# Three transformer layers on one core: spreads issued in mid-tile, small steps regrouped, and the first two out projections in rounds over pairs of inputs

## The reference, cut to what matters

```python
memn = rms_norm(mem, mem_norm_w)
for layer in range(2):
    u = rms_norm(x, attn_norm_w[layer]) @ w_in[layer]            # 1024 -> 2560
    if layer == 0:   # chunked retention, 6 heads, group norm, silu gate
        o_main = silu(g) * rms_norm(retention(q, k, v), ret_gn_w)
    else:            # differential attention: two softmax maps a head
        q, k = rms_norm(q, ...), rms_norm(k, ...)
        o = softmax(q0 k0) - lam * softmax(q1 k1), times v
        o_main = rms_norm(o, diff_subln_w) * (1 - lambda_init)
    o_mem = memory_attention(rms_norm(qc), rms_norm(mk), mv)     # mk, mv from memn @ w_mem_kv
    x = x + concat(o_main, o_mem) @ w_out[layer]                 # 1024 -> 1024
    h = rms_norm(x, ffn_norm_w[layer]) @ w_gate_up[layer]        # 1024 -> 2 * 2816
    x = x + (silu(h[:2816]) * h[2816:]) @ w_down[layer]
# layer 2: Mamba-2 scan (16 heads, 4-tap convolution) beside forgetting attention (16 heads)
proj = rms_norm(x, norm_mix_w) @ w_in_2                          # 1024 -> 5664
x = x + concat(ssd_mixer(...), fox_mixer(...)) @ w_out_2         # 2048 -> 1024
x = x + (silu(gate) * val) @ w_down_2   # gate, val = conv3(rms_norm(x) @ w_up_2)
```

## Time and profile before

| | before |
|---|---|
| median of three runs | 1100.18 us (1098.59 to 1103.19) |
| the profiled execution's own time | 1097.26 us |
| its span in the profile | 1095.5 us |
| PE busy | 1052.4 us, 96% |
| DVE busy | 760.9 us, 69% |
| ACT busy | 586.6 us, 54% |
| POOL busy | 178.8 us, 16% |
| mean granted clock of TensorE | 0.995 of full |
| read from HBM | 172.39 MB |

### The profile page before, as it was taken

One profiled execution on the slowest core, in us unless ns is written; L12 is line 12 of the kernel. 1 busy time (PEld: TensorE's weight loads), 2 busy tenths in 40 slices (PEclk: granted clock), 3 DMA queues, 4 the chain that ended last, 5 costly groups with the idle time before them and its releaser, 6 DMA issues.

```text
span 1095.5 us, 23936 instructions
## 1 busy us (share of the span) xinstructions
PE 1052.4 (96%) x8666; PEld 1013.2 (92%) x8666; DVE 760.9 (69%) x1323; ACT 586.6 (54%) x1047; POOL 178.8 (16%) x186
## 2 busy tenths in 40 slices
PE   5999999999999998999999999989899999999998
PEld 5989999999999877899999999988788999999998
DVE  6876686666555887866666459857877679988843
ACT  6654564444544645654445446655555566666532
POOL 4100121111110000411111110000212023444300
PEclk9999999999999999999999999999999999999999
DMA  7533455555565321555555654433232455555563
GB/s 279 179 134 106 144 175 185 180 180 179 178 194 165 124 88 53 189 178 186 184 180 176 194 184 141 172 115 136 78 116 71 133 196 179 175 188 176 167 208 103
DMA packets 51480, 174.45 MB, mean 159 GB/s; under 512 B 5840, under 2 KB 7120, under 8 KB 51280
## 3 DMA queue, kind: packets, MB, share of 16 engines
q1 hardware_dynamic: 51408, 173.46, 47.5%
HBM read 172.39 MB, written 1.05 MB: 158 GB/s over the span
## 4 chain that ended last, share of the span: by engine, by line
PE 80%; DVE 14%; ACT 3%; issue 2%; POOL 1%; DMA 1%; SPq 0%; DVEq 0%; POOLq 0%; ACTq 0%
PE bank L678 23%; PE bank L679 23%; PE bank L680 23%; DVE ring_lo L1447 4%; DVE xw_lo L1453 1%; ACT tmp L1212 1%; PE bank L663 1%; PE bank L665 1%; PE bank L664 1%; PE bank L788 1%; ACT tmp L1269 1%; PE bank L879 1%; PE bank L977 1%; DVE root_parts L1651 1%; PE bank L899 1%
## 5 line engine op out<-in xcount | busy, mean ns | idle before, releaser
L678 PE MATMUL bank<-xw_hi,ring_hi 128*128 128x256 f32 x1576 | 452.0, 287 | 2.6 <-ACT lam L1347 1.1
L679 PE MATMUL bank<-xw_lo,ring_hi 128*128 128x256 f32 x1576 | 446.0, 283 | 0.0
L680 PE MATMUL bank<-xw_hi,ring_lo 128*128 128x256 f32 x1576 | 445.8, 283 | 0.0
L1447 DVE TENSOR_TENSOR ring_lo<-ring_raw,ring_hi 128x1024 fp32r<-128x1024 f32 (+2 forms) x338 | 402.3, 1194 | 57.9 <-ACT ring_hi L1031 52.2
L1031 ACT ACTIVATE ring_hi<-ring_raw 128x1024 fp32r<-128x1024 f32 (+2 forms) x338 | 341.2, 1012 | 90.5 <-PE bank L680 84.5
L678 PEld LDWEIGHTS bank<-xw_hi,ring_hi 128*128 128x128 f32 x1576 | 302.3, 192 | 8.3 <-issue 3.7
L679 PEld LDWEIGHTS bank<-xw_lo,ring_hi 128*128 128x128 f32 x1576 | 302.4, 192 | 0.2
L680 PEld LDWEIGHTS bank<-xw_hi,ring_lo 128*128 128x128 f32 x1576 | 302.3, 192 | 0.0
L678 PE MATMUL bank<-act_hi,ring_hi 128*128 128x256 f32 x736 | 211.6, 288 | 11.0 <-DVE ring_lo L1853 7.5
L679 PE MATMUL bank<-act_lo,ring_hi 128*128 128x256 f32 x736 | 209.3, 284 | 0.0
L680 PE MATMUL bank<-act_hi,ring_lo 128*128 128x256 f32 x736 | 209.2, 284 | 0.0
(11 more groups left out here) (193 smaller groups left out, 1180.6 us busy)
## 6 DMA issues: line engine op xcount, KB each, us to landing
ring_raw<-w_up SPq DMA_DIRECT2D x132, 512.0 KB, 3.2
ring_raw<-w_in SPq DMA_DIRECT2D x85, 512.0 KB, 3.2
ring_raw<-w_down SPq DMA_DIRECT2D x48, 512.0 KB, 3.5
ring_raw<-w_down SPq DMA_DIRECT2D x24, 384.0 KB, 3.8
ring_raw<-w_ob SPq DMA_DIRECT2D x10, 512.0 KB, 3.8
ring_raw<-w_oa SPq DMA_DIRECT2D x16, 256.0 KB, 2.6
ring_raw<-w_oa SPq DMA_DIRECT2D x8, 512.0 KB, 3.6
ring_raw<-w_kv SPq DMA_DIRECT2D x7, 512.0 KB, 6.9
```

What stands on the lines that cost most here:

```text
L678: mm(bank[b][:, 0:T], w_hi, tile(hi, t), start=kk == 0, stop=False)
L679: mm(bank[b][:, 0:T], w_hi, tile(lo, t), start=False, stop=False)
L680: last = mm(bank[b][:, 0:T], w_lo, tile(hi, t), start=False, stop=end)
L1447: V.tensor_tensor(ring_lo[:, a:b], ring_raw[:, a:b], ring_hi[:, a:b].bitcast(f32), SUB).then_inc(lo_done, 1)
```

## The change

Seven things are changed.

1. In layers 0 and 1 the phases oa and ob become one phase oc of eight rounds (`project_rounds`). Round (pair, half) multiplies one pair of inputs into four outputs; the order is (0,0), (1,0), (0,1), (1,1), (2,0), (2,1), (3,0), (3,1), with the pairs (6,7), (0,1), (2,3), (4,5). All eight sums lie two to a bank in banks 0 to 3, and x gets them in four additions of 512 columns in rounds 6 and 7.
2. In layer 1 most spreads, in layer 2 all spreads and `ssd_out`, are issued in the middle of the next tile (`amid`). Spreads of layer 1 named `spread_soon` stay where they were. In DVE's EARLY list of those layers `ssd_skip` and `norm_out` come last.
3. `ssd_out` reads one of four buffers (`ssd_w`), so ACT may be two pairs ahead.
4. At the start ACT splits kv tile 1 before the first square; POOL adds six squares, PE itself sums the last two, after kv tile 2; kv weights are split one tile further ahead, and three tiles of x are split before the kv loop.
5. Plan: gate_silu and gated of layer 0 one slot earlier, the last norm of layer 1 one slot earlier, its last mixes at slot 25.
6. Lambda's sums and exponential move to slot 1 of layer 0.
7. `small_r` holds its 256 columns in doubled order (512 columns, in `act_hi`), so that the broadcasts of the scan and of the forgetting attention take one matmul of 384 columns and not two of 256 and 128.

```diff
-          ("in0", 20, [8], 20), ("oa0", 8, [6], 8), ("ob0", 2, [8], 2), ("up0", 44, [8], 4), ...
-          ("in1", 20, [8], 20), ("oa1", 8, [4], 8), ("ob1", 4, [8], 4), ("up1", 44, [8], 4), ...
+          ("in0", 20, [8], 20), ("oc0", 8, [8], 8), ("up0", 44, [8], 4), ...
+          ("in1", 20, [8], 20), ("oc1", 8, [8], 8), ("up1", 44, [8], 4), ...
+ROUNDS = [(0, 0), (1, 0), (0, 1), (1, 1), (2, 0), (2, 1), (3, 0), (3, 1)]
...
-        plan[layer][slot + 2].insert(0, ("spread", tile))
+        plan[layer][slot + 2].insert(0, ("spread_soon" if soon or slot >= 20 and layer == 1 else "spread", tile))
...
-    norm(1, 23, 10 + 64, True)
+    norm(1, 22, 10 + 64, True)
...
         def ssd_w(h):
-            return tmp[:, 1920 + (h % 2) * 384:2304 + (h % 2) * 384]
+            room, a = (tmp, 1920) if h % 4 < 2 else (con, CCOL["dist"])
+            return room[:, a + (h % 2) * 384:a + 384 + (h % 2) * 384]
...
+        X_SPLITS = {1: (3,), 2: (4, 5), 3: (6,), 4: (7,)}
+        X_SQUARES = {1: (0, 1), 2: (2, 3), 3: (4, 5), 4: (6, 7)}
...
+            def project_rounds(layer, then, halfway):
+                ph = PH[f"oc{layer}"]
+                for c, (pair, half) in enumerate(ROUNDS):
+                    slot, g = ph.tile(0, c)
+                    pe.wait_ge(lo_done, g + 1)
+                    ...
+                    for j in range(4):
+                        if j == 2:
+                            halfway(c)
+                        m = 4 * half + j
+                        b = m // 2
+                        ...
+                        o = bank[b][:, (m % 2) * T:(m % 2) * T + T]
+                        for k in range(2):
+                            t = ph.inputs[2 * pair + k]
+                            if m == 0:
+                                pe.wait_ge(mix_lo, number["mix", (layer, t)] + 1)
+                            ...
+                        if pair == 3 and j == 1:
+                            last.then_inc(ob_done, 1)
+                    last.then_inc(tile_done, 1)
+                    then(c)
...
+                if q == 0:
+                    mm(bank[7][:, 0:T], cmat("ones1024"), sqsum, start=True, stop=False)
+                    pe.wait_ge(sq_done, KT)
+                    for r in (KT - 2, KT - 1):
+                        last = mm(bank[7][:, 0:T], cmat("ones1024"), two(sq, r % 2), start=False, stop=r == KT - 1)
...
-                    if c == (1 if name == "kv" else 0) and q is not None:
+                    if c == (2 if name == "kv" else 0) and q is not None:
                         mean_square(q)
...
-                    for it, a, width in blocks_:
-                        mm(bank[2 + n][:, a:a + width], pick, small_r[:, 0:width], start=it == 0, stop=False)
+                    mm(bank[2 + n][:, 0:T + P], pick, small_r[:, 0:T + P], start=True, stop=False)
...
+            HALFWAY = ((), ("spread",), ("spread", "ssd_out"))
...
-                if layer == 1:
-                    pe.wait_ge(lam_in, 1)
-                    mm(bank[5][:, 0:2], ...).then_inc(lam_ps, 1)
-                    pe.wait_ge(lam_e, 1)
...
             for g in range(1, AHEAD):
                 split_hi(PH["kv"], 0, g - AHEAD)
-                for m in range(3 * g - 1, 3 * g + 2):
+                for m in range(4 * g - 4, 4 * g):
                     stream_square(0, m, u)
+                    for k in {5: (0, 1), 6: (2,)}.get(m, ()):
+                        act.wait_ge(x_loaded, 16)
+                        stream_hi(1, k, x)
...
+            def rounds_into_stream(layer, q, early, middle, late):
+                ph = PH[f"oc{layer}"]
+                for c in range(ph.n):
+                    early(ph, 0, c)
+                    if c >= 6:
+                        for p in (2 * c - 12, 2 * c - 11):
+                            ...
+                            V.tensor_tensor(two_out, two_out, bank[p][:, :], ADD).then_inc(out_ready, 1)
+                            if p:
+                                stream_lo(q, 2 * p - 2, x)
+                                stream_lo(q, 2 * p - 1, x)
+                    ...
+                    split_lo(ph, 0, c)
+                    late(ph, 0, c)
```

229 lines of the change are left out of this document (153 added, 76 removed), and 4 rows, old and new, of the table PHASES.

## The result

| | before | changed |
|---|---|---|
| median of five runs each, us | 1100.18 (1098.43 to 1103.19) | 1088.51 (1086.83 to 1090.04) |
| ratio | | 0.9891, 95% interval 0.9868 to 0.9913 |
| profiled execution, us | 1097.26, span 1095.5 | 1086.83, span 1085.0 |
| PE busy, us | 1052.4 | 1050.0 |
| PE idle, us | 43.1 | 35.0 |

The change is faster by 11.7 us in the medians (10.5 in the profiles). I had predicted 1077 us, a gain of 21.6, with a range that ended at 1088. The direction was right, and about half of the gain is missing.

A forecast was written before the change was run, and what follows sets the result against it. PE was taken to bound the kernel, busy 1052.4 of 1095.5 us. Gains of 1.5 + 3.8 + 1.1 + 5.2 + 2.3 + 6.5 + 1.2 = 21.6 us took the profiled 1097.26 to 1075.7; median predicted 1077, range 1070 to 1088.

The forecast's parts named there:

- The start, 1.5: Kv phase: without PE's wait for POOL's sums, kv tile 3 starts at 21.0, not 22.5; gain 1.5 us, bounds 0 and 2.7.
- Out projection of layer 0, 3.8: Start of layer 0's out projection: a 2.08 us wait for split inputs and a 1.7 us clock loss go; gain 3.8 us.
- Up0 stays as it is: Start of layer 0's up projection: unchanged within 0.7 us either way, wide additions saving DVE a little, later order costing a little.
- Lambda, 1.1: Start of layer 1: PE's wait for lambda goes as its work moves to layer 0; gain 1.1 us, lower bound 0.
- Layer 1, 5.2: Layer 1: spreads 3.4, softmax 1.4, clock 0.9, mixes 0.5, less about 1.0 at up1; net gain 5.2 us, bounds 1.5 and 9.5.
- The clock, 3.5 in three terms: Half-speed stretches in layers 0, 1 and 2: gains of 1.7, 0.9 and 0.9 us from less slow clock, 3.5 in all.
- the clock stays: Rival: all three half-speed stretches return, 3.5 us less gain, 1080.5 us; chance 0.10.
- Layer 2, 10.0: Layer 2: 2.3 us from the long `ssd_out` wait and clock, 6.5 from other `ssd_out` and spread waits, 1.2 from broadcasts.
- Broadcasts, 1.2: Layer 2's broadcasts: merging the attention's matmuls saves 0.15 us for each of eight head pairs, 1.2 us; bounds 0 and 1.5.
- Slower by the half tile as DVE's wait: Rival: 23 deferred steps in layers 1 and 2 each give PE its bank up to 1.44 us later; worst 1123 us; chance 0.05.
- DVE takes over: Rival: in layers 1 and 2 waits return behind DVE's one queue, 7.0 us less gain, 1084 us; chance 0.18.
- Rounds still wait for mixes: Rival: layer 1's rounds wait for late mixes, each wait bringing a clock stretch, 6.4 us less gain, 1083 us; chance 0.07.

The follow-up runs named there:

- u_kv: m_all4 with the start as before (splits and squares of x beside the first four kv tiles, POOL summing all eight squares); 1077.01 us.
- c_lo: Changed kernel with DVE's low half of the weight tile in round 6 computed ahead of that round's two additions, layers 0 and 1; 1085.26 us.
- f_half1: Changed kernel with layer 1's spread matmuls back at the end of their tile; 1091.63 us.
- a_bank: Changed kernel with the out projection rounds' four PSUM banks taken in order 1, 0, 2, 3, in both layers; 1087.57 us.
- b_mix: Changed kernel with layer 1's mixes of head pair 2, 3 put ahead of the last RMS norm's root in slot 23; 1086.33 us.
- d_all: Changed kernel with the edits of a_bank, b_mix and c_lo together; 1079.71 us.
- o_fill: Changed kernel with 18 unused matmuls filling PE's waits in the first tile of up0 and of up1; 1086.68 us.
- t_bcast: m_all4 with layer 2's broadcasts, for decays and attention, in two matmuls each again; 1075.45 us.
- s_ssdend: k_nosort with layer 2's `ssd_out` back at the tile's end, its spreads still in mid-tile; 1096.75 us.
- k_nosort: Changed kernel with DVE's early steps of layer 2 in the plan's order, `norm_out` no longer sorted to the end; 1083.92 us.
- m_all4: Changed kernel with all four repairs: the edits of a_bank, b_mix, c_lo and k_nosort; 1074.24 us.
- j_norounds_bank: Changed kernel with both out projections by output as before, first output in the bank the last input tile has not used; 1086.91 us.
- g_half2: Changed kernel with layer 2's spreads and `ssd_out` back at the end of their tile; 1099.29 us.
- h_kv: Changed kernel with the start as before (splits and squares of x beside the first four kv tiles, POOL summing all eight squares); 1091.66 us.

## Why the prediction was wrong

By the two marks and the spans, in us of the profiled executions (with the repairs the marks stand at 340.40 and 650.10, the span is 1072.6):

| | forecast | changed | with the four repairs |
|---|---|---|---|
| start and layer 0, lambda among it | 6.4 | 2.9 | 5.4 |
| layer 1 | 5.2 | -1.5 | 4.4 |
| layer 2 | 10.0 | 9.1 | 13.1 |
| sum | 21.6 | 10.5 | 22.9 |
| of it clock | 3.5 | 0 | 5.1 |

The time fell the way that was forecast, but by 11.7 us and not 21.6, and landed just above the range. Two things failed: the terms of layer 1 and of the start of up0, which left out what stands ahead in the other engines' queues, and the clock's 3.5 us, of which none came. With the four repairs the waits give 17.8 us without the clock, against 18.1 forecast, so the places for the gain were there.

- **The start, 1.5.** By the first spread 0.8 (48.47 to 47.69). Mis-sized, inside its bounds. Kv tile 3 began at 21.31, near the 21.0 of the sum; what I had not seen is a wait of 0.57 for a low part at 36.97 that before did not have. On medians the new start is worth 2.8 to 3.2, since the wait that it removes can bring stretches of slow clock; in the one run of u_kv with a granted clock of 1.00 it is 0.7.
- **Out projection of layer 0, 3.8.** Oc0 began without the wait and without the stretch, as said. What failed is "Up0 stays as it is": from its first matmul to the mean it took 6.8 us (140.19 to 146.97) against 4.5. The order of DVE's queue in round 6, which I had put at "within 0.7 either way", cost more than half of the term, and a stretch came there. c_lo shows it: start and layer 0 are 2.3 us shorter with the order changed, 1.7 of it that stretch.
- **Lambda, 1.1.** Right: the row is gone.
- **Layer 1, 5.2, the step that failed.** It lost 1.5. The softmax's wait went to 0.3, better than the 1.0 of the sum. Its spreads were worth 1.5 and not 3.4, by f_half1 without the clock; the median's 3.1 is near by luck. The half tile of cover took the spreads' waits away, but one of them, 1.83, came back as the norm's 1.90. Three more things were wrong. I had not looked at which bank round 0 begins in (2.3 us). I let the mixes wait 0.5 and they waited 2.0: not POOL's 3.41 us was at fault but the norm ahead of the mixes in ACT's queue, put there by the slot that the change moved the norm to. And up1's first tile took 7.0 us (456.99 to 463.99), not 4.5. These last three are shown by a_bank, b_mix and c_lo together, d_all: layer 1 falls from 315.7 to 309.7 us.
- **The clock, 3.5 in three terms.** Three stretches went and three came. The rival "the clock stays" had this right with its 3.5 us. The Trainium skill ("TensorE: Matmul & The Clock Gate", HAM oscillation) describes an array that falls back in the waits between groups of matmuls. Every stretch here did follow waits, and in o_fill none came where they were filled; the stretches at 411 and 424 show that a wait alone does not tell whether one comes.
- **Layer 2, 10.0.** 9.1 by the marks, and near by luck: two errors cancel. On the medians the mid-tile steps are worth 14.0 and not the 8.8 that I gave them, but 5.0 of it is clock; the rest, 9.1, is near the 7.9 of the sum (1.4 + 6.5). The sort of DVE's list, which I had not priced at all, cost 4.0 by the marks (4.6 on the medians). My sum of separate waits, 2.3 for `ssd_out` and 6.5 for the rest, is not how they divide: spreads alone bring nothing that is clear of noise.
- **Broadcasts, 1.2.** Right as a sum, by t_bcast; by the rows 0.10 a pair and not 0.15. By the Trainium skill's issue gap alone it would have been 0.1 ("TensorE: Matmul & The Clock Gate", Back-to-back issue gap), and the same section says that this formula under-counts for matmuls of few columns, since it leaves out the loading of the weights; the measured 1.2 decides for the rows.
- **Rivals.** "Slower by the half tile as DVE's wait" did not come. "DVE takes over" is seen as a mechanism in s_ssdend, in the norm's 1.90 us of layer 1 and in the norms' waits behind the sorted list, but the last comes by the order of its queue and not by DVE being full: k_nosort and m_all4 have the same work on DVE and no such wait in layer 2. "Rounds still wait for mixes" had the right place in layer 1, with 2.0 us and a stretch. "The clock stays" was right about the clock, and its 1080.5 wrong since it kept the other terms.
- **What was to show it.** PE busy fell by 2.4, within 5; the idle time is 35 and not 25; the spreads' rows are under 2.5 and `ssd_out` under 2. Kv tile 3 began without the wait of about 1 that I had named.

What stays open: why the same wait has a stretch at half speed in one run and none in another, what `ssd_out` in mid-tile brings without the spreads, and whether rounds or the old order are better in layer 1 once both have the right bank.

## What to carry to other kernels

When work is regrouped on the engine that sets the time, write down for each boundary what the other engines have in their queues just before the first thing that it needs: the bank it starts in, the norm ahead of its mixes, the weight split between its sums. The four losses that were repaired here were each one thing in the wrong place, a bank or an order in a queue; none was missing throughput. Waits on one queue move: here moving one of two steps that depend on the same engine brought nothing clear of noise, since the other's waits grew by about as much, and moving both brought 9.1 us, 14.0 with the clock. And compare variants by the marks of the part that was edited, beside the granted clock: medians that differ by one or two stretches can point the wrong way, as in j_norounds_bank.

## What the runs showed of the hardware

- A stretch at half speed was 3.4 us long or twice that, and took 1.7 or 3.4 us from PE. The profiles of the change and its eighteen variants have between none (m_all4) and seven (g_half2, h_kv) of them, a long one counted twice, behind single waits of 1.06 to 3.32 us or rows of short ones, the least of them 0.36 and three of 0.26 (u_kv at 456 us; m_all4 has the same row and no stretch).
- A stretch that took 1.7 us from PE cost the kernel nothing where a wait for DVE stood behind it (t_bcast, 408 to 412 us). An edit in one layer moved stretches in another: k_nosort, whose layers 0 and 1 are those of the changed kernel, has twice the stretch at 145 to 151 us. With up to 1.7 us per stretch, the medians of neighbouring variants tell less than the marks in their traces. The five runs of m_all4 agreed within 0.5 us, at granted clocks of 1.00 and 0.998.
- DVE's low part of a weight tile (128x1024) took 1.77 us at 139.41 and 1.23 us at 133.18; in the first case POOL was adding squares (138.40 to 141.75). In c_lo it moved to a time when POOL was idle and took 1.23.
- At the start matmuls of 256 columns began 0.21 us apart, the pace of the stretches at half speed, while the granted clock reads 1.00; the clock's sums leave that out.
